# Split products from the tenth early block on, six more blocks ahead of the gates, and the last two Gelus left in PSUM

## The chip, the core and the metric

The kernel runs on one core of a Trainium2 chip. The metric is the device time of one execution in microseconds (us); of three executions of the kernel before, the median is 944.98 us. TensorE is called PE here, VectorE DVE, ScalarE ACT, GpSimd POOL and the queue that issues the DMAs SP, as in the profile.

## What is computed

One transformer layer on 256 tokens: attention and a pooling mixer, a projection, and then a feed-forward part with 16,384 experts, which takes most of the time. The reference of that part, cut:

```python
s1 = einsum('bthd,nd->bthn', q1, sub_keys1); s2 = einsum('bthd,nd->bthn', q2, sub_keys2)
v1, i1 = top_k(s1, 16); v2, i2 = top_k(s2, 16)           # per head, 8 heads, 128 keys each
cand_s = v1[..., :, None] + v2[..., None, :]             # 256 candidates
cand_i = i1[..., :, None] * 128 + i2[..., None, :]
top_s, pos = top_k(cand_s, 16); eid = take_along_axis(cand_i, pos)
gate = softmax(top_s)
a = gelu(einsum('td,tkd->tk', h, peer_u[eid]))
out = einsum('tk,tkd->td', gate * a, peer_v[eid])
```

The kernel gathers nothing: it computes `gelu(h @ peer_u.T)` for all experts, multiplies it with a matrix of gates that is zero where an expert was not picked, and multiplies by all of `peer_v`.

## The kernel before, in words

The experts are cut into 128 blocks of 128. A block has an *up* half (its 128 x 1024 part of `peer_u` times the normed tokens, then Gelu) and a *down* half (the gated result times its part of `peer_v`, 12 matmuls of 512 columns, `down`). The first 108 blocks (`EARLY`) have their up half done early, before the gates exist, and their Gelus are kept in DRAM (`up_dram`) until the down stage reads them back. The other 20 have it done in the late loop, between the down halves (`up`).

An up half comes in two forms. In *full precision* (`early_part`, line 1975) the matmul is fp32. As a *split product* the weights and the tokens are each a high part (a rounded copy) plus a low part (the rest), and three products of them are summed: high by high, high by low, low by high. A narrow split block is 24 matmuls of 256 columns (`split_part`, line 2045), a wide one 8 of 512 and 8 of 256 columns. The high part of a block's weights is a copy by ACT (`early_high`, line 759), the low part a subtraction by DVE or POOL (`early_low`, lines 1325 and 1642). The tokens' own low parts (`low_part` in POOL, line 1558, four pieces, semaphore `p_hlo`) are needed too.

Between 140 and 235 us the *picks* are made, head by head, for 8 heads. PE makes the scores. DVE finds the best keys (`best_keys`, line 1216 and on) and the best pairs (`best_pairs`), compares positions (line 1247), and sums up the expert numbers (`look_up`, line 1255). POOL adds up candidates (`candidates`, `staircase`, line 1563) and multiplies matches by numbers (`matches`, line 1593). `last_matches` (line 1266) is DVE's share of the eighth head's matches; it waits for `p_cide`, which POOL sets after its last staircase. Seven small steps follow in DVE, and then PE transposes the picks (line 2064). PE fills this time with early blocks: 0 to 12 in full precision, 13 and 14 (`SPLIT_E`) as split products.

After that the *gates* are built by one-hot products (`gate_half`, line 2077), with the split blocks 14 to 107 woven in by a fixed count of matmuls (`fill`). Then comes the down stage: 108 down halves, and the late loop.

All of it is in an order written out by hand: each engine runs its own list, and waits on named counters. `e_up` counts finished up halves, `e_gel` Gelus, `eu_hi` and `eu_lo` high and low parts of weights. SP loads each block's weights into a ring of three (`load_ring`, `ld_t`), stores each Gelu (`store_early`), and itself waits in its list for these counters. A Gelu goes into one of two `gel` buffers, and so waits for the store of two blocks before:

```python
act.wait_ge(e_up, e + 1)
if e >= 2:
    act.wait_ge(st_e[e % 2], 16 * (e // 2))
act.activation(gel[:, e % 2, :], psum[:, early_bank(e), 0:SEQ], ACT.Gelu).then_inc(e_gel, 1)
```

## Time and profile before

| | us |
|---|---|
| median of 3 executions | 944.98 (943.74 to 945.27) |
| the profiled execution | 942.8 |
| its span | 941.0 |
| PE busy | 932.4 |
| DVE busy | 770.6 |
| ACT busy | 500.3 |
| POOL busy | 321.2 |

The span runs from the first to the last instruction of the execution; the time of the execution is 1.8 us longer. The granted clock of PE is 1.00 over the whole trace behind its first microseconds. Matmuls are pipelined, so what a block costs is read from the start of one group of matmuls to the start of the next, not from durations.

### The profile page before, as it was taken

The numbers are of one execution on the slowest core, as the hardware profiler recorded it, in microseconds if no ns is written. First come the engines' busy times: TensorE is split into PE (matmuls) and PEld (weight loads), VectorE is DVE, ScalarE is ACT, GpSimd is POOL, SyncE is SP. The second block draws the span as 40 slices with busy tenths as digits, with TensorE's granted clock in tenths as the row PEclk, the third lists the DMA queues.
The fourth block names the chain that finished last, engine by engine and source line by source line (L and its number), as shares of the span: only waits on it lengthen the run. The fifth ranks groups of instructions, "written<-read, shape, count | busy, mean of one in ns | idle before, by whom it ended". The sixth has DMA issues, their size and how long they took to land.

```text
span 941.0 us, 15375 instructions
## 1 busy us (share of the span) xinstructions
PE 932.4 (99%) x5396; PEld 816.7 (87%) x5396; DVE 770.6 (82%) x1450; ACT 500.3 (53%) x872; POOL 321.2 (34%) x292
## 2 busy tenths in 40 slices
PE   9999999999999999999999999999999999999998
PEld 8998899998988888888888888888888888888887
DVE  5899758999886888788778898888888888777776
ACT  6576544433767777777777544334343343343342
POOL 3084228888476766767667000000000000000000
PEclk9999999999999999999999999999999999999999
DMA  9543138826776676667667777787777777766664
GB/s 293 160 135 123 48 99 300 211 78 179 216 245 198 206 218 195 226 195 236 203 200 224 250 246 232 245 242 236 245 236 243 239 237 245 206 219 186 195 193 140
DMA packets 93783, 193.46 MB, mean 206 GB/s; under 512 B 8449, under 2 KB 59265, under 8 KB 93457
## 3 DMA queue, kind: packets, MB, share of 16 engines
q1 hardware_dynamic: 93280, 190.38, 64.8%
q0 software_dynamic: 288, 2.10, 1.2%
q8 instruction: 40, 0.66, 0.3%
q14 instruction: 31, 0.25, 0.1%
q10 hardware_dynamic: 144, 0.08, 0.0%
HBM read 174.43 MB, written 15.99 MB: 202 GB/s over the span
## 4 chain that ended last, share of the span: by engine, by line
PE 95%; ACT 2%; DVE 2%; DMA 1%; issue 0%; DVEq 0%; ACTq 0%
PE psum L2131 37%; PE psum L2051 16%; PE psum L2048 8%; PE psum L1675 5%; PE psum L1975 5%; PE psum L1944 4%; PE psum L2111 4%; PE psum L2077 3%; PE psum L2045 2%; PE psum L1691 2%; PE psum L2114 2%; PE psum L1732 1%; PE psum L1853 1%; PE psum L1969 1%; PE psum L1936 1%; DMA up_kept<-gel 1%
## 5 line engine op out<-in xcount | busy, mean ns | idle before, releaser
L2131 PE MATMUL psum<-rr 128*128 128x512 f32 x1536 | 354.0, 390 | 1.0 <-DVE rr L1399 1.0
L2131 PEld LDWEIGHTS psum<-rr 128*128 128x128 f32 x1536 | 286.0, 188 | 64.6 <-issue 1.1
L851 ACT ACTIVATE rr<-raw 128x1024 fp32r<-128x1024 f32 x105 | 111.7, 1064 | 176.4 <-PE psum L2131 176.2
L1332 DVE TENSOR_TENSOR rr<-raw,rr 128x1024 fp32r<-128x1024 f32 x106 | 129.9, 1225 | 25.9 <-ACT rr L851 25.5
L2051 PE MATMUL psum<-h_all,rr 128*128 128x512 f32 x456 | 123.4, 395 | 0.0
L2051 PEld LDWEIGHTS psum<-h_all,rr 128*128 128x128 f32 x456 | 82.5, 188 | 13.5
L1352 DVE TENSOR_REDUCE gel<-psum 128x256 f32<-128x512 f32 x86 | 58.6, 681 | 14.3 <-DMA up_kept<-gel 12.7
L759 ACT ACTIVATE rr<-raw 128x1024 fp32r<-128x1024 f32 x64 | 67.2, 1050 | 4.7 <-DMA raw<-in_peer_u_dram 4.6
L2051 PE MATMUL psum<-h_all,late_b 128*128 128x512 f32 x232 | 64.8, 394 | 0.0
L1635 POOL TENSOR_TENSOR rr<-raw,h_all 128x640 fp32r<-128x640 bf16 x32 | 40.3, 1259 | 59.0 <-DVE raw L1309 58.7
L1399 DVE TENSOR_TENSOR rr<-big,rr 128x256 fp32r<-128x256 f32 x128 | 54.4, 425 | 4.4
L889 ACT ACTIVATE rr<-raw 128x1024 fp32r<-128x1024 f32 x22 | 23.4, 1062 | 62.0 <-PE psum L2131 61.1
L1393 DVE TENSOR_TENSOR big<-big,gel 128x256 f32<-128x256 f32 (+1 forms) x128 | 53.6, 419 | 2.8 <-ACT gel L750 2.0
L2111 PE MATMUL psum<-h_all,rr 128*128 128x512 f32 x152 | 54.4, 392 | 0.0
L1397 DVE TENSOR_SCALAR rr<-big 128x256 fp32r<-128x256 f32 (+1 forms) x128 | 37.7, 294 | 20.2 <-PE psum L2131 9.7
L845 ACT ACTIVATE big<-psum 128x512 f32<-128x512 f32 x64 | 37.8, 591 | 29.5 <-PE psum L2077 29.3
L745 ACT ACTIVATE gel<-gel 128x256 f32<-128x256 f32 x86 | 35.3, 411 | 31.5 <-DVE gel L1352 30.5
L1635 POOL TENSOR_TENSOR rr<-raw,picks 128x640 fp32r<-128x640 bf16 x32 | 49.1, 1536 | 0.0
L2051 PEld LDWEIGHTS psum<-h_all,late_b 128*128 128x128 f32 x232 | 42.9, 188 | 6.7
L1385 DVE TENSOR_TENSOR rr<-raw,rr 128x1024 fp32r<-128x1024 f32 x22 | 26.9, 1225 | 25.9 <-ACT rr L889 25.9
L1675 PE MATMUL psum<-rr,h_all 128*128 128x256 f32 (+1 forms) x384 | 46.5, 281 | 0.6 <-ACT raw L612 0.6
L1975 PE MATMUL psum<-t32s,raw 128*128 128x256 f32 x208 | 46.7, 379 | 0.0
(240 smaller groups left out, 1766.5 us busy)
## 6 DMA issues: line engine op xcount, KB each, us to landing
raw<-in_peer_v_dram SPq DMA_DIRECT2D x128, 512.0 KB, 3.9
raw<-in_peer_u_dram SPq DMA_DIRECT2D x127, 512.0 KB, 4.2
up_kept<-gel SPq DMA_DIRECT2D x106, 128.0 KB, 3.6
gel<-up_kept SPq DMA_DIRECT2D x106, 128.0 KB, 3.9
big<-in_w_in_dram SPq DMA_DIRECT2D x10, 1024.0 KB, 5.7
big<-in_peer_wq_dram SPq DMA_DIRECT2D x8, 1024.0 KB, 5.5
big<-in_w_out_dram SPq DMA_DIRECT2D x4, 1024.0 KB, 5.3
rr<-big POOLq DMA_DIRECT2D x2, 1024.0 KB, 8.9
```

The lines of the kernel that those rows point to most:

```text
L759: act.activation(early_split(e, 0), u_ring[e % 3].rearrange("p (k n) -> p k n", k=DK), ACT.Copy).then_inc(eu_hi, 1)
L851: act.activation(v_sp[b % 2][:, 0, :], early_v(b), ACT.Copy).then_inc(v_hi, 1)
L1332: dve.tensor_tensor(v_sp[b % 2][:, 1, :], early_v(b), f(v_sp[b % 2][:, 0, :]), ALU.subtract).then_inc(v_lo, 1)
L1352: dve.tensor_reduce(gel[:, e % 2, :], psum[:, early_bank(e), :].rearrange("p (a t) -> p t a", a=2), AX.X, ALU.add).then_inc(e_sum, 1)
L1399: dve.tensor_tensor(g_sp[:, s, 1, :], gates_at(b), f(g_sp[:, s, 0, :]), ALU.subtract).then_inc(g_lo, 1)
L1635: i = pool.tensor_tensor(pairs_at[q % 2][:, 0:n, part, :], cols[q % 2][:, :, :, 0], p.unsqueeze(2).to_broadcast([P, n, NK]), ALU.mult)
L1675: i = pe.matmul(dst, lhs(a, k), rhs(b, k), start=(n == 0), stop=(n == 3 * DK - 1))
L1975: i = pe.matmul(psum[:, early_bank(e), 0:SEQ], u_ring[e % 3][:, k * P:(k + 1) * P], t32s[:, k, :], start=(k == 0), stop=(k == DK - 1))
L2048: i = pe.matmul(bank[:, 0:SEQ], early_split(e, 1)[:, k, :], ht[:, 0, k, :], start=False, stop=False)
L2051: i = pe.matmul(bank.rearrange("p (a t) -> p a t", a=2), early_split(e, 0)[:, k, :], ht[:, :, k, :], start=(k == 0), stop=(k == DK - 1))
L2111: return pe.matmul(both, ut[s][:, 0, k, :], ht[:, :, k, :], start=(k == 0), stop=(k == DK - 1))
L2131: i = pe.matmul(psum[:, 4 + 2 * t + n, :], g_sp[:, s, x, t * P:(t + 1) * P], v_sp[s][:, y, n * 512:(n + 1) * 512], start=(first and m == 0 ...
```

## The change

`EARLY` goes from 108 to 114 and `EARLY_TOP` from 15 to 21: six blocks leave the late loop, and 21 blocks stand ahead of the gates. From block 9 on (`SPLIT0`) all early blocks are split products, so that 9 to 12 change their form and 13 to 18 are new there. The blocks woven between the gates are 94 before and after. What goes with it:

- PE computes blocks 0 to 8 in full precision, 9 to 18 with `split_part`, then as before one block around the transposes. Each of them waits for the Gelu of the block two before (`e_gel`). In block 9 the order of products is changed, so that the token's low parts are needed last.
- ACT copies the tokens' high part one step earlier (in the last head's turn, ahead of `keep_s`), and makes the high parts of blocks 9 to 20 between its Gelus.
- DVE makes the low parts of blocks 9 to 20, between the steps of the picks' last two heads.
- POOL makes the tokens' four low parts ahead of the matches of the sixth head; before, one came after those matches and three after the last.
- SP loads blocks 9 to 11 into space left by the projections' weights (`raw_more`), ahead of time, and 12 on into the ring; from block 12 on a load waits for a low part.
- The last two Gelus (blocks 112 and 113) are written in place in PSUM, and DVE multiplies from there; so they wait for no store, and SP can reload the first two stored Gelus into `gel` as soon as the stores are done.

The core of the diff:

```diff
-EARLY, EARLY_TOP = 108, 15
+EARLY, EARLY_TOP = 114, 21
+SPLIT0 = PH + 1
-EXP_AT = EARLY_TOP - 5
+EXP_AT = SPLIT0 + 4
...
+        raw_more = [wraw.rearrange("p s k n -> p (s k n)")[:, n * D:(n + 1) * D] for n in range(3)]
-        early_sp = [rr[:, n:n + 2 * D].rearrange("p (a k n) -> p a k n", a=2, k=DK) for n in (2 * D, 4 * D)]
+        early_sp = [rr[:, n:n + 2 * D].rearrange("p (a k n) -> p a k n", a=2, k=DK) for n in (2 * D, 4 * D, 6 * D, 0)]
...
             def keep_early(e):
                 sp.wait_ge(e_up, e + 1)
-                load_ring(e + 3)
+                if e < SPLIT0 - 3:
+                    load_ring(e + 3)
+                else:
+                    sp.wait_ge(ld_t[e % 3], 16 * (e // 3 + 2))
+                    load_ring(e + 6)
                 if e:
                     store_early(e - 1)
+                if e == SPLIT0 - 4:
+                    sp.wait_ge(z_done, z_after(N_CHUNK - 1))
+                    for k in range(3):
+                        sp.wait_ge(ld_t[k], 16 * ((SPLIT0 - 3) // 3 + 1))
+                        load_ring(SPLIT0 + k)
...
                 act.wait_ge(e_up, e + 1)
+                if e >= EARLY - 2:
+                    mine = psum[:, early_bank(e), 0:SEQ]
+                    act.activation(mine, mine, ACT.Gelu).then_inc(e_gel, 1)
+                    return
...
+                if h == PH - 1:
+                    act.wait_ge(p_t32, 1)
+                    act.activation(ht[:, 0], t32s, ACT.Copy).then_inc(a_hi, 1)
                 keep_s(h)
...
+            early_high(SPLIT0)
+            early_high(SPLIT0 + 1)
             numbers(PH - 1)
             for e in range(PH - 1, EXP_AT):
                 early_gelu(e)
+                if e < SPLIT0:
+                    early_high(e + 4)
+                elif e > SPLIT0:
+                    early_high(e + 3)
...
                 if h < PH:
                     best_keys(h)
+                if h == PH - 1:
+                    early_low(SPLIT0)
...
                 if h >= 2:
                     best_pairs(h - 1)
+                if h == PH - 1:
+                    early_low(SPLIT0 + 1)
                 if h == PH:
...
                     last_matches()
+                    early_low(SPLIT0 + 4)
                 if h >= 2:
                     look_up(h - 2)
+                if h == PH - 1:
+                    early_low(SPLIT0 + 2)
+                    early_low(SPLIT0 + 3)
+            for e in range(SPLIT0 + 5, SPLIT0 + 8):
+                early_low(e)
             dve.wait_ge(d_seq, seq.n)
             look_up(PH - 1)
+            early_low(SPLIT0 + 8)
...
-            for e in SPLIT_E:
+            for e in range(SPLIT0 + 9, FILL0 + 1):
                 early_low(e)
...
+                if h == PH - 2:
+                    for n in range(N_OUT):
+                        low_part(n)
                 matches(h - 1)
-                if h == PH - 2:
-                    low_part(0)
-            for n in range(1, N_OUT):
-                low_part(n)
...
-            for e in range(PH - 2, EARLY_TOP - 2):
+            for e in range(PH - 2, SPLIT0):
                 early_up(e)
...
                     if n == 0:
                         pe.wait_ge(eu_hi, split_number(e))
+                        if e < FILL0:
+                            pe.wait_ge(e_gel, e - 1)
...
-            pe.wait_ge(e_gel, EARLY_TOP - 3)
             pe.wait_ge(a_hi, 4)
-            pe.wait_ge(p_hlo, N_OUT)
+            for e in range(SPLIT0, SPLIT_E[0]):
+                split_part(e, 0, UNITS)
             split_part(SPLIT_E[0], 0, 2 * DK)
```

In the lists below a row is one instruction with its line, the tile it writes, what it reads, and the counters it waits for. DVE at the end of the picks, before: `L1282` is the step ahead of `last_matches` (`L1266`), `L1255` is `look_up`, `L1290` the first of the small steps, `L1325` a low part of a block's weights.

```order
L1282 TENSOR_TENSOR big<-big 128x256
L1266 TENSOR_TENSOR big<-big 128x800 [waits p_cide,d_match]
L1255 TENSOR_REDUCE big<-big 128x2x16 [waits p_eq]
L1255 TENSOR_REDUCE big<-big 128x2x16 [waits p_eq,d_seq]
L1290 CAST big<-big 128x256 [waits d_pick]
```

The same place after the change, where `L1327`, `L1307`, `L1290` and `L1342` are these steps and `L1300` is a low part:

```order
L1327 TENSOR_TENSOR big<-big 128x256
L1307 TENSOR_TENSOR big<-big 128x800 [waits p_cide,d_match]
L1300 TENSOR_TENSOR rr<-raw,rr 128x1024 [waits eu_hi]
L1290 TENSOR_REDUCE big<-big 128x2x16 [waits p_eq]
L1300 TENSOR_TENSOR rr<-raw,rr 128x1024 [waits eu_hi] x3
L1290 TENSOR_REDUCE big<-big 128x2x16 [waits p_eq,d_seq]
L1300 TENSOR_TENSOR rr<-raw,rr 128x1024 [waits eu_hi]
L1342 CAST big<-big 128x256 [waits d_pick]
```

The low part of block 13 now stands right behind `last_matches`, those of 14 to 16 behind the first `look_up`, that of 17 behind the second. Four more (9 to 12) stand earlier in the same list.

POOL around the matches of the sixth head, before: `L1563` is the end of a staircase, `L1593` and `L1605` the matches, `L1558` a low part of the tokens.

```order
L1593 TENSOR_TENSOR big<-big 128x800 [waits d_match,p_cide,p_seq]
L1593 TENSOR_TENSOR big<-big 128x800
L1605 TENSOR_TENSOR big<-big 128x2x400 [waits p_seq]
L1558 TENSOR_TENSOR h_all<-t32s,h_all 128x2x256 [waits a_hi]
L1563 TENSOR_TENSOR big<-big 128x2x16 [waits d_top]
```

After the change, with `L1607` as the low parts and `L1612`, `L1642`, `L1654` as staircase and matches:

```order
L1607 TENSOR_TENSOR h_all<-t32s,h_all 128x2x256 [waits a_hi] x4
L1612 TENSOR_TENSOR big<-big 128x2x16 [waits n_ev]
...
L1642 TENSOR_TENSOR big<-big 128x800 [waits d_match,p_cide,p_seq]
L1642 TENSOR_TENSOR big<-big 128x800
L1654 TENSOR_TENSOR big<-big 128x2x400 [waits p_seq]
L1612 TENSOR_TENSOR big<-big 128x2x16 [waits d_top]
```

All four low parts of the tokens now stand ahead of the sixth head's staircase and matches.

## Rows read from the trace of the kernel before

**Rows 1.** The page: busy us (share of span) x instructions of each engine.

```profile
PE 932.4 (99%) x5396; PEld 816.7 (87%) x5396; DVE 770.6 (82%) x1450; ACT 500.3 (53%) x872; POOL 321.2 (34%) x292
```

**Rows 2.** PE's waits, longest first: who waited, for whom: us, times, longest.

```profile
PE psum L1719 <- POOL big L1467: 1.0, 1, 1.0
PE psum L2131 <- DVE rr L1399: 1.0, 1, 1.0
```

**Rows 3.** Timeline of PE ahead of the gates: start, us, instruction, [idle before <-releaser].

```profile
208.66 24.34 PE L1975 MATMUL psum<-t32s,raw 128*128 128x256 f32 x112
232.65 2.24 PE L2045 MATMUL psum<-h_all,rr 128*128 128x256 f32 x16
...
245.99 3.01 PE L2045 MATMUL psum<-h_all,late_b 128*128 128x256 f32 x24
248.83 1.10 PE L2045 MATMUL psum<-h_all,rr 128*128 128x256 f32 x8
```

**Rows 4.** Timeline of PE in the late loop.

```profile
829.99 2.91 PE L2131 MATMUL psum<-rr 128*128 128x512 f32 x12
832.73 0.40 PE L2111 MATMUL psum<-h_all,rr 128*128 128x512 f32 x1
...
835.51 2.91 PE L2131 MATMUL psum<-rr 128*128 128x512 f32 x12
```

**Rows 5.** Timelines of PE, ACT and DVE at the start of the down stage.

```profile
527.53 2.97 PE L2045 MATMUL psum<-h_all,late_b 128*128 128x256 f32 x24
531.47 38.76 PE L2131 MATMUL psum<-rr 128*128 128x512 f32 x169 [0.96 <-DVE rr L1399]
...
529.62 0.39 ACT L750 ACTIVATE gel<-psum 128x256 f32<-128x256 f32 x1 [0.96 <-DMA up_kept<-gel]
...
530.11 0.43 DVE L1393 TENSOR_TENSOR big<-big,gel 128x256 f32<-128x256 f32 x1 [1.97 <-ACT gel L750]
```

**Rows 6.** Timeline of POOL in the last three heads of the picks.

```profile
215.44 1.28 POOL L1558 TENSOR_TENSOR h_all<-t32s,h_all 128x512 fp32r<-128x512 f32 x1
...
222.97 2.10 POOL L1563 TENSOR_TENSOR big<-big 128x32 f32<-128x32 f32 x7
225.20 2.37 POOL L1593 TENSOR_TENSOR big<-big 128x800 f32<-128x800 bf16 x1
227.53 3.75 POOL L1558 TENSOR_TENSOR h_all<-t32s,h_all 128x512 fp32r<-128x512 f32 x3
```

**Rows 7.** Timeline of DVE at the end of the picks.

```profile
225.17 0.99 DVE L1266 TENSOR_TENSOR big<-big 128x800 f32<-128x800 bf16 x1 [0.66 <-POOL big L1563]
226.08 5.72 DVE L1255 TENSOR_REDUCE big<-big 128x32 f32<-128x1600 f32 x2
231.83 0.30 DVE L1290 CAST big<-big 128x256 int32<-128x256 f32 x1
...
234.24 2.35 DVE L1325 TENSOR_TENSOR rr<-raw,rr 128x1024 fp32r<-128x1024 f32 x2
```

**Rows 8.** Timelines of DVE and POOL where they work on SBUF at once.

```profile
190.36 2.82 DVE L936 TENSOR_TENSOR rr<-big,rr 128x2048 fp32r<-128x2048 f32 x1 [1.48 <-ACT rr L552]
238.71 2.31 DVE L1325 TENSOR_TENSOR late_c<-raw,rr 128x1024 fp32r<-128x1024 f32 x1
...
189.49 5.11 POOL L1593 TENSOR_TENSOR big<-big 128x800 f32<-128x800 bf16 x2
...
201.27 3.06 POOL L1593 TENSOR_TENSOR big<-big 128x800 f32<-128x800 bf16 x2
...
238.68 1.26 POOL L1635 TENSOR_TENSOR rr<-raw,picks 128x640 fp32r<-128x640 bf16 x1
```

**Rows 9.** Timelines of SP (issue of a weight load) and ACT in the picks.

```profile
226.13 0.33 SPq L436 DMA_DIRECT2D raw<-in_peer_u_dram  x1
...
224.10 1.28 ACT L811 ACT_TABLE_LOAD   x1
229.75 1.06 ACT L759 ACTIVATE rr<-raw 128x1024 fp32r<-128x1024 f32 x1 [0.64 <-DMA raw<-in_peer_u_dram]
```

**Rows 10.** Timeline of PE in the first microseconds.

```profile
1.00 3.44 PE L1719 MATMUL psum<-big 128*128 128x128 f32 x16 [1.00 <-POOL big L1467]
...
6.04 0.83 PE L1719 MATMUL psum<-big 128*128 128x128 f32 x6
```

More of the change, by code:

```diff
@@ L372, in early_split, with early_raw @@
         def early_split(e, part):
-            return early_sp[e - SPLIT_E[0]][:, part] if e in SPLIT_E else split_ring[e % 3][part]
+            return early_sp[(e - SPLIT_E[0]) % 4][:, part] if e <= FILL0 else split_ring[e % 3][part]
+        def early_raw(e):
+            return raw_more[e - SPLIT0] if SPLIT0 <= e < SPLIT0 + 3 else u_ring[e % 3]
         def split_number(e):
-            return e - SPLIT_E[0] + 1
+            return e - SPLIT0 + 1
         def split_low_ready(eng, e):
-            mine = [k for k in range(SPLIT_E[0], e + 1) if pool_low(k) == pool_low(e)]
+            mine = [k for k in range(SPLIT0, e + 1) if pool_low(k) == pool_low(e)]
             eng.wait_ge(ep_lo if pool_low(e) else eu_lo, len(mine))
@@ L469, in _ @@
             load_w(WQ0 + 6)
-            for e in range(SPLIT_E[0]):
+            for e in range(SPLIT0):
                 keep_early(e)
@@ L476, in _ @@
                     load_w(WQ0 + 7)
-            for e in range(SPLIT_E[0], EARLY):
+            for e in range(SPLIT0, EARLY):
                 keep_split(e)
@@ L481, in _ @@
             sp.dma_start(u_first.rearrange("p k n -> p (k n)"), pu[EARLY]).then_inc(ld_uf, 16)
+            for b in range(2):
+                sp.wait_ge(st_e[b], 8 * (EARLY - 2))
+                load_e(b + 2)
             for b in range(EARLY):
-                sp.wait_ge(d_g32, b + 1)
-                if b < 2:
-                    sp.wait_ge(st_e[b], 8 * (EARLY - 2))
-                if b < EARLY - 2:
+                if 2 <= b < EARLY - 2:
+                    sp.wait_ge(d_g32, b + 1)
                     load_e(b + 2)
@@ L758, in early_high @@
                     act.wait_ge(e_up, e - 2)
-                act.activation(early_split(e, 0), u_ring[e % 3].rearrange("p (k n) -> p k n", k=DK), ACT.Copy).then_inc(eu_hi, 1)
+                elif e >= SPLIT0 + 4:
+                    act.wait_ge(e_up, e - 3)
+                act.activation(early_split(e, 0), early_raw(e).rearrange("p (k n) -> p k n", k=DK), ACT.Copy).then_inc(eu_hi, 1)
             def numbers(h):
@@ L801, in _ @@
                     early_gelu(h - 2)
-            act.wait_ge(p_t32, 1)
-            act.activation(ht[:, 0], t32s, ACT.Copy).then_inc(a_hi, 1)
             early_gelu(PH - 2)
@@ L877, in _ @@
                         early_next(e)
+                if c == HALVES - 1:
+                    ring_v(1)
                 if q < NQ:
@@ L1260, in block_u, with early_low @@
                 dve.tensor_tensor(ut[s][:, 1], u_raw[:, s], f(ut[s][:, 0]), ALU.subtract).then_inc(ut_lo, 1)
+            def early_low(e):
+                dve.wait_ge(eu_hi, split_number(e))
+                dve.tensor_tensor(early_split(e, 1), early_raw(e).rearrange("p (k n) -> p k n", k=DK), f(early_split(e, 0)), ALU.subtract)\
+                   .then_inc(eu_lo, 1)
             def last_matches():
@@ L1344, in next_rows @@
             def next_rows(q):
+                if q == 0:
+                    dve.wait_ge(e_up, FILL0 - 2)
                 if q >= RS:
@@ L1392, in block_g @@
                     dve.wait_ge(a_gel, b + 1 - EARLY)
-                dve.tensor_tensor(gates_at(b), gates_at(b), gel[:, s, :], ALU.mult).then_inc(d_g32, 1)
+                up_gelu = psum[:, early_bank(EARLY - 2 + b), 0:SEQ] if early and b < 2 else gel[:, s, :]
+                dve.tensor_tensor(gates_at(b), gates_at(b), up_gelu, ALU.mult).then_inc(d_g32, 1)
                 dve.wait_ge(d_g32, b + 1)
@@ L2040, in split_part @@
                             pe.wait_ge(e_gel, e - 2)
-                    if n == (2 * DK - 2 if wide(e) else 2 * DK):
+                    if e == SPLIT0 and n == 2 * DK:
+                        pe.wait_ge(p_hlo, N_OUT)
+                    if n == (DK if e == SPLIT0 else 2 * DK - 2 if wide(e) else 2 * DK):
                         split_low_ready(pe, e)
```

25 lines of the change are left out of this document (14 added, 11 removed).

## The prediction

> **What bounds the kernel now.** I read the page's busy line first: TensorE (PE) is busy 932.4 of 941.0 us [rows 1]. Then PE's waits: none is longer than 1.0 us, and after the start the longest is that before the first block of the down stage [rows 2]. So PE has work behind work from end to end; an edit gains only by giving PE less of it or by taking out that 1.0 us, and it loses by whatever makes PE wait anew. After that I read the timelines of PE, VectorE (DVE), GpSimd (POOL) and ScalarE (ACT) between 205 and 245 us, where the picks are made, since all of the moved work lands there. The reader should see two things in them: VectorE and GpSimd are both without a gap there, and they hand results to and fro.
>
> **PE's own work.** A block in full precision is 16 matmul records. Seven of them run from 208.66 to 232.65 [rows 3], so one costs 23.99/7 = 3.43 us. A narrow split block is 24 matmuls of 256 columns: 245.99 to 248.83, 2.84 us [rows 3]. An up block in the late loop takes 832.73 to 835.51 = 2.78 us, the down half 829.99 to 832.73 = 2.74 us [rows 4]. By the diff four blocks (9 to 12) go from full precision to split, and six blocks leave the late loop and are computed ahead of the gates as narrow blocks. The 86 wide blocks stay 86, and the blocks woven between the gates stay 94. So PE loses 4 x 3.43 + 6 x 2.78 = 30.4 us and gets 10 x 2.84 = 28.4 us: -2.0 us. All of it lies on PE, which sets the end, so all of it counts. The moved blocks' down halves do not change; their extra store and reload of 128 KB run on queues in which PE does not wait today.
>
> **The start of the down stage.** PE ends its fill at about 530.5 (527.53 plus 24 matmuls) and starts at 531.47 [rows 5]. What came last is ScalarE's Gelu of block 106, which waited 0.96 us for a store to free its `gel` buffer [rows 5]. With the result left in PSUM it waits for no store and can start at about 528.6, behind ScalarE's copy of v; VectorE's three steps behind it (1.2 us, 530.11 to 531.3 today) then end before PE is there. I take the whole 0.96 us: -0.9. If VectorE's reads from PSUM cost more, up to all of it is lost (0).
>
> Together -2.9 us, if nothing new waits. The rest of the working is about that.
>
> **When PE wants the low parts.** Nothing before block 9 moves on PE, so block 9 starts at 208.66 + 3 x 3.43 = 218.95, and block 13 at 218.95 + 4 x 2.84 = 230.3. Its last eight matmuls need its low part, 16 matmuls later: at 232.2.
>
> **When VectorE can have it.** The low part of block 13 stands behind `last_matches`, which waits for GpSimd's last `p_cide`. Today that comes at 222.97 + 2.10 = 225.07 [rows 6], and VectorE had waited 0.66 us for it [rows 7]. GpSimd's work up to there is one unbroken line, and the change puts things into it:
> - Three of its four low parts of the tokens move from behind the matches to ahead of them: 3.75 us [rows 6]. That makes 228.8. (The fourth lay in the line before, at 215.44 [rows 6].)
> - VectorE's four new low parts (blocks 9 to 12). Rows 8 show what a subtraction of two SBUF tiles on VectorE does beside a GpSimd instruction: one waits for the other to end. A subtraction that came at 190.36 in the middle of GpSimd's pair of 800-element products made the pair last 5.11 us where another pair lasts 3.06; a low part at 238.71 lasted 2.31 us, waiting for the GpSimd product that had begun at 238.68, where two low parts in a row last 2.35 us together with nobody beside them [rows 7, 8]. So each low part among GpSimd's line holds that line up by its own length, some 1.15 us: 4 x 1.15 = 4.6. That makes 233.4.
>
> From there the order of today's rows goes on: `last_matches` takes 0.9 us; GpSimd's last product, already waiting, goes next and ends 2.5 us after `p_cide` (225.07 to 225.20 + 2.37 [rows 6]), and the low part, 1.2 us, comes behind it: 233.4 + 2.5 + 1.2 = 237.1. PE wanted it at 232.2, so PE waits about 5.0 us. This takes in the smaller waits of blocks 9 and 10 for their low parts, which push block 13 back but not the chain.
>
> The low part of block 14 stands behind `look_up` of the seventh head, half of 5.72 us [rows 7]: it comes 2.86 + 1.15 = 4.0 us after that of block 13, and PE asks 2.84 us after: +1.2. Blocks 15 to 17 follow 1.15 us apart or have time. The end of the chain (`look_up`, the low part of 17, the seven small steps) comes 2 x 1.15 + 2.86 + 1.15 + 2.4 = 8.7 us after the low part of 14, while PE reaches the transposes 0.95 + 4 x 2.84 + 1.9 = 14.2 us after it; that wait stays hidden.
>
> Bounds of the new waits: none if VectorE and GpSimd held each other up nowhere (below); at the top, 8.7 us, if the moved low parts of GpSimd also hold up the comparisons of VectorE that run at the same time (two, by 1.25 us each: +2.5). I take 6.2, because rows 8 show the hold-up on just these kinds of instruction, and GpSimd's line has no gap to hide it.
>
> The Trainium skill, "SBUF — State Buffer", section "Who interferes with whom", goes further than the rows: it says that any VectorE instruction with two SBUF inputs shuts out a GpSimd instruction that reads SBUF for its whole length, and the other way round. By that VectorE's comparisons of 800 bf16 elements would wait for GpSimd's low parts as well, which no row shows, as they only met the staircase's instructions of 0.3 us (2.10/7 [rows 6]); the sum by it would be up to 2.5 us more.
>
> **Sum.** -2.0 - 0.9 + 5.0 + 1.2 = +3.3 us. The profiled execution took 942.8 us (span 941.0 and 1.8 around it), 2.2 under the median of 944.98; by the profile the new time is 946.1, and against the median 944.98 + 3.3 = 948.3.
>
> **Rivals.**
> - *The chain has room (faster).* If the two engines passed each other freely, GpSimd's line ends at 228.8 and VectorE, today ready for `last_matches` at 225.17 - 0.66 = 224.5, is ready at 224.5 + 4.6 = 229.1: block 13's low part is there at 231.2, a microsecond ahead of PE. What then comes last is ScalarE: the Gelu of block 13 stands behind the load of block 15 (3.6 us from issue to use, 226.13 to 229.75), its copy and two table loads of 1.28 us [rows 9]; the load goes out at about 228.1, so 228.1 + 3.6 + 1.06 + 1.28 + 0.42 + 1.28 + 0.39 = 236.1, and PE asks at 218.95 + 6 x 2.84 = 236.0. That is up to 0.8 us with the stores. -2.9 + 0.8 = -2.1: 942.9. The decision lies at 232.2: the low part of block 13 before or after. Against it: rows 8, and a GpSimd line that has no gap.
> - *Half of it (no change to be seen).* The low parts fall where GpSimd waits for its own results, and take the memory in time that it doesn't use; how many such moments there are, the merged rows do not show. Half of the 4.6 us gone leaves waits of 2 to 4 us: -0.9 to +1.1, about 945.0.
> - *PE's clock falls in the wait.* A wait of 5 us in PE is longer than any in the trace. Its price by rows: at the start, before the clock was granted, 16 matmuls took 3.44 us, and six of the same kind later 0.83 [rows 10]; 3.44 - 16 x 0.83/6 = 1.2 us once, 949.5. The records of this run show no level below full speed after the start, so whether 5 us is enough is open. The Trainium skill, "TensorE: Matmul & The Clock Gate", Part 1, says that an idle PE is gated to half rate again; no row here shows it.
>
> **How the numbers follow.** A measurement of this kernel can tell about 0.2%, 1.9 us, from no change. The hold-up in the chain, with or without the clock: 0.62, slower, 947 to 952. Half of it: 0.20, within 0.2%. Room in the chain: 0.18, faster, 942.9. The forecast is that of the first, 948.3. The range goes from 943.0, which leaves out about half of the last case, to 952.0: -2.9 + 8.7 + 1.2 = +7.0 at the top end.
>
> **What would show it.** In the profile after: PE's waits list a single wait of 4 to 6 us on VectorE's low part of block 13, and one of about 1 us on that of block 14; GpSimd's last `p_cide` ends near 233 and not 225; its pairs of 800-element products last 4 to 5 us where a low part falls between them; the first gate starts 20.9 us later than now (10 x 2.84 - 4 x 3.43 = 14.7 of it work, 6.2 waits). In the down stage the wait of 1.0 us is gone and the late loop is 6 x 2.78 = 16.7 us shorter. The forecast is wrong if low part 13 ends ahead of 232.2, if VectorE's low parts do not lengthen GpSimd's line, or if narrow blocks in this stretch take other than 2.84 us.

## The result and the profile after

The changed kernel takes 947.95 us (median of 8 executions, 946.33 to 949.45), the kernel before 944.62 beside it: a ratio of 1.0035 (95% interval 1.0026 to 1.0045), 3.3 us slower. In a second series the same two kernels gave 946.3 and 943.3, ratio 1.0030 (1.0019 to 1.0041). The profiled execution of after took 948.26 us, 0.3 over its median, while the profiled one of before lies 1.8 under its own; so two profiles laid side by side show more than 3.3.

| start of | before | after | after, second series |
|---|---|---|---|
| first fp32 matmul of the early blocks | 154.22 | 155.02 | 154.35 |
| first gate | 240.79 | 263.19 | 261.56 |
| last gate | 526.47 | 549.59 | 548.23 |
| down stage | 531.47 | 553.46 | 552.10 |
| its last matmul | 937.33 | 942.80 | 941.57 |

All differences below are taken from one start to the next, so what an execution had lost ahead of the early blocks drops out. From the first early block to the first gate the changed kernel takes 21.6 us more (20.6 in the second series); the prediction said 20.9. The gates take 0.7 and 1.0 more, the start of the down stage 1.1 less, the down stage with the late loop 16.5 and 16.4 less: in sum +4.7 and +4.1 against a profile of before that was a short one.

PE's waits in the profile of after (who waited, for whom: us, times, longest), to be laid beside [rows 2], and its timeline (start, us, instruction, [idle before <- releaser]) beside [rows 3]:

```profile
PE psum L2098 <- DVE rr L1300: 3.6, 2, 3.1
...
PE psum L2098 <- ACT gel L776: 0.9, 1, 0.9
```

```profile
209.46 10.53 PE L2022 MATMUL psum<-t32s,raw 128*128 128x256 f32 x48
220.94 1.17 PE L2098 MATMUL psum<-h_all,rr 128*128 128x256 f32 x8 [0.95 <-ACT gel L776]
222.65 12.88 PE L2098 MATMUL psum<-h_all,rr 128*128 128x256 f32 x104 [0.54 <-DVE rr L1300]
238.59 18.91 PE L2098 MATMUL psum<-h_all,rr 128*128 128x256 f32 x144 [3.06 <-DVE rr L1300]
257.34 0.82 PE L2117 MATMUL psum<-cst,big 128*128 128x128 f32 x6
```

Block 9 waits for a Gelu, then for its low part, and at 235.5 block 13 waits 3.06 us for its low part. The last group but one holds a further loss that no list of waits shows: 144 matmuls take 18.75 us to the next group's start, where six times 2.84 us for 24 [rows 3] is 17.0. The granted clock says why (stretch, length, PE busy, PEclk, DMA share, GB/s; after):

```profile
236.00:238.00 2.00, 0.00 (x0) 1.00 0.01 4
238.00:240.00 2.00, 1.41 (x9) 0.81 0.25 41
240.00:242.00 2.00, 2.00 (x11) 0.50 0.76 283
242.00:244.00 2.00, 2.00 (x17) 0.84 0.25 51
244.00:246.00 2.00, 2.00 (x20) 1.00 0.75 278
```

It is 1.00 through the wait, falls to 0.50 (1.2 of 2.4 GHz) shortly after PE has started again, and is back at 1.00 by 244. The three stretches below 1.00 lose 2 x (0.19 + 0.50 + 0.16) = 1.7 us.

VectorE and GpSimd in the picks of after (timelines), to be laid beside [rows 6 to 8]:

```profile
209.55 1.28 DVE L1279 CAST big<-big 128x32 bf16<-128x32 uint32 x1
210.86 3.15 DVE L1282 TENSOR_TENSOR big<-big 128x800 bf16<-128x800 bf16 x2
...
220.06 2.53 DVE L1300 TENSOR_TENSOR rr<-big,rr 128x1024 fp32r<-128x1024 f32 x1
...
229.28 2.58 DVE L1300 TENSOR_TENSOR rr<-raw,rr 128x1024 fp32r<-128x1024 f32 x1
233.53 0.18 DVE L1279 CAST big<-big 128x32 bf16<-128x32 uint32 x1
233.75 1.06 DVE L1282 TENSOR_TENSOR big<-big 128x800 bf16<-128x800 bf16 x2
...
235.06 2.34 DVE L1307 TENSOR_TENSOR big<-big 128x800 f32<-128x800 bf16 x1
237.32 1.21 DVE L1300 TENSOR_TENSOR rr<-raw,rr 128x1024 fp32r<-128x1024 f32 x1
```

```profile
209.53 5.63 POOL L1607 TENSOR_TENSOR h_all<-t32s,h_all 128x512 fp32r<-128x512 f32 x4 [0.32 <-ACT h_all L820]
...
216.48 3.06 POOL L1642 TENSOR_TENSOR big<-big 128x800 f32<-128x800 bf16 x2
...
221.47 4.20 POOL L1612 TENSOR_TENSOR big<-big 128x32 f32<-128x32 f32 x14
225.80 4.97 POOL L1642 TENSOR_TENSOR big<-big 128x800 f32<-128x800 bf16 x2
230.74 2.22 POOL L1612 TENSOR_TENSOR big<-big 128x32 f32<-128x32 f32 x7
234.98 1.57 POOL L1642 TENSOR_TENSOR big<-big 128x800 f32<-128x800 bf16 x1 [2.03 <-DVE big L1282]
```

Read them in pairs, the lines of VectorE with those of GpSimd that run at the same time. Beside GpSimd's four token low parts (209.53 on) VectorE's copy of 32 elements takes 1.28 us, undisturbed 0.18, and its two comparisons 3.15, undisturbed 1.06. Two of the new low parts take 2.5 us, undisturbed 1.2. The other way round GpSimd's pair of products takes 4.97 us beside low parts, undisturbed 3.06, and its last seven staircase steps 2.22, where they take 1.24 in the run with one source, below. The kernel before had a sign of it that is in none of the rows ahead of the prediction: beside GpSimd's products the last head's copy took 0.68 us, in the two heads ahead of it 0.23 and 0.25 (timeline of DVE, before):

```profile
222.37 0.68 DVE L1244 CAST big<-big 128x32 bf16<-128x32 uint32 x1
```

The last `p_cide` comes at 232.96, or at 232.2 with the 0.8 us taken off by which this execution runs behind (predicted 233.4). In this execution VectorE is later still: GpSimd then waits 2.03 us for VectorE's comparisons. In the second series the end is as predicted, although there the low parts hold up the staircase (14 steps in 6.22 us) and not the pair of products (3.07 us): the last `p_cide` comes at 233.19, `last_matches` waits 0.83 us for it, GpSimd's product goes next, and low part 13 is there at 236.8 (predicted 237.1; GpSimd, then VectorE, second series):

```profile
221.73 6.22 POOL L1612 TENSOR_TENSOR big<-big 128x32 f32<-128x32 f32 x14
...
231.11 2.08 POOL L1612 TENSOR_TENSOR big<-big 128x32 f32<-128x32 f32 x7
233.32 2.37 POOL L1642 TENSOR_TENSOR big<-big 128x800 f32<-128x800 bf16 x1
...
233.29 0.99 DVE L1307 TENSOR_TENSOR big<-big 128x800 f32<-128x800 bf16 x1 [0.83 <-POOL big L1612]
234.20 2.57 DVE L1300 TENSOR_TENSOR rr<-raw,rr 128x1024 fp32r<-128x1024 f32 x1
```

At the down stage (timelines of ACT and PE, to lay beside [rows 5]) the Gelu waits for no store, and PE starts without a wait:

```profile
551.35 0.38 ACT L772 ACTIVATE psum<-psum 128x256 f32<-128x256 f32 x1
...
553.46 2.91 PE L2184 MATMUL psum<-rr 128*128 128x512 f32 x12
```

### The profile page after: what moved, and what is told of

The parts are those of the page before. It is cut to its first block, busy times and chain, and to the rows that moved or that the text cites. A ratio compares the mean times of both kernels' runs of the same rounds, so it can differ in the third digit from the quotient of the medians.

```text
span 946.5 us, 15438 instructions
## 1 busy us (share of the span) xinstructions
PE 934.5 (99%) x5476; PEld 821.2 (87%) x5476; DVE 772.8 (82%) x1448; ACT 505.4 (53%) x876; POOL 328.2 (35%) x292
## 4 chain that ended last, share of the span: by engine, by line
PE 68%; DVE 3%; DMA 2%; issue 1%; ACT 1%; POOL 1%; SPq 0%; DVEq 0%; ACTq 0%
PE psum L2184 37%; PE psum L2104 15%; PE psum L2101 8%; PE psum L2130 3%; PE psum L2164 3%; DMA up_kept<-gel 2%; PE psum L2167 1%; PE psum L2098 1%; DVE late_c L1300 1%; DVE rr L1300 0%; ACT rr L787 0%; DVE big L1290 0%; PE psum L1722 0%; DVE big L1510 0%; POOL rr L1682 0%
## 5 line engine op out<-in xcount | busy, mean ns | idle before, releaser
L886 ACT ACTIVATE rr<-raw 128x1024 fp32r<-128x1024 f32 x111 | 118.0, 1063 | 186.0 <-PE psum L2184 186.0
L1378 DVE TENSOR_TENSOR rr<-raw,rr 128x1024 fp32r<-128x1024 f32 x112 | 137.2, 1225 | 27.3 <-ACT rr L886 26.7
L2104 PE MATMUL psum<-h_all,rr 128*128 128x512 f32 x456 | 123.4, 395 | 0.0
L2104 PEld LDWEIGHTS psum<-h_all,rr 128*128 128x128 f32 x456 | 82.5, 188 | 13.5
L787 ACT ACTIVATE rr<-raw 128x1024 fp32r<-128x1024 f32 x71 | 74.6, 1051 | 2.0 <-DMA raw<-in_peer_u_dram 1.9
L2098 PE MATMUL psum<-h_all,rr 128*128 128x256 f32 x392 | 50.6, 287 | 4.7 <-DVE rr L1300 3.6
L1300 DVE TENSOR_TENSOR rr<-raw,rr 128x1024 fp32r<-128x1024 f32 x26 | 38.3, 1480 | 20.1 <-ACT rr L787 20.1
L1446 DVE TENSOR_SCALAR rr<-big 128x256 fp32r<-128x256 f32 (+1 forms) x128 | 37.7, 294 | 20.6 <-PE psum L2184 13.4
L2098 PEld LDWEIGHTS psum<-h_all,rr 128*128 128x128 f32 x392 | 48.8, 194 | 5.8 <-DVE rr L1300 4.3
L1682 POOL TENSOR_TENSOR rr<-raw,picks 128x640 fp32r<-128x640 bf16 x32 | 52.1, 1628 | 0.0
L1722 PEld LDWEIGHTS psum<-rr,h_all 128*128 128x128 f32 (+1 forms) x384 | 44.5, 176 | 2.0 <-issue 1.0
L1372 DVE TENSOR_TENSOR big<-psum,big 128x512 f32<-128x512 f32 x64 | 43.5, 680 | 2.3 <-ACT big L880 2.2
```

What stands on the lines that cost most here:

```text
L787: act.activation(early_split(e, 0), early_raw(e).rearrange("p (k n) -> p k n", k=DK), ACT.Copy).then_inc(eu_hi, 1)
L886: act.activation(v_sp[b % 2][:, 0, :], early_v(b), ACT.Copy).then_inc(v_hi, 1)
L1378: dve.tensor_tensor(v_sp[b % 2][:, 1, :], early_v(b), f(v_sp[b % 2][:, 0, :]), ALU.subtract).then_inc(v_lo, 1)
L1682: i = pool.tensor_tensor(pairs_at[q % 2][:, 0:n, part, :], cols[q % 2][:, :, :, 0], p.unsqueeze(2).to_broadcast([P, n, NK]), ALU.mult)
L1722: i = pe.matmul(dst, lhs(a, k), rhs(b, k), start=(n == 0), stop=(n == 3 * DK - 1))
L2098: i = pe.matmul(bank[:, 0:SEQ], early_split(e, x)[:, k, :], ht[:, y, k, :], start=(n == 0), stop=(n == UNITS - 1))
```

## The experiments

The theory was that of the prediction: VectorE and GpSimd hold each other up on SBUF, and that makes low part 13 late. The main rival was that VectorE's own added time (four low parts of 1.15 us) does it. Ratios are to the kernel before, run on the same chip, with 95% intervals. The waits are those of the profiled execution: "Gelu" is a wait for a Gelu, "low 13" one for the low part of block 13, and "slow clock" says that the granted clock fell to 0.50 behind the wait.

| run | ratio | PE's waits ahead of the gates, us |
|---|---|---|
| changed kernel again (r_after) | 1.0030 (1.0019 to 1.0041) | Gelu 1.1, low 13 3.0, slow clock |
| one-source low parts (e3_onesrc) | 0.9988 (0.9979 to 0.9997) | Gelu 1.3, low 13 1.2, low 14 0.9 |
| token low parts late (e4_tokens) | 0.9999 (0.9990 to 1.0008) | Gelu 1.1, low 13 1.3, low 14 1.0 |
| both (e34_both) | 0.9978 (0.9968 to 0.9987) | Gelu 0.2, low 13 0.2, low 14 1.0 |
| two low parts sooner (e2_order) | 1.0004 (0.9995 to 1.0012) | Gelus 1.3 and 0.9, low parts 0.2, 0.9, 0.4 |
| filled wait (e5_clock) | 1.0034 (1.0022 to 1.0045) | Gelu 1.7, low 14 0.4 |
| Gelus in PSUM alone (e1_gelu) | 0.9997 (0.9989 to 1.0006) | none |
| tokens by DMA (e7_dma) | 1.0069 (1.0055 to 1.0083) | DMA 7.7, slow clock, Gelu 0.5 |
| and reordered (e8_best) | 1.0058 (1.0044 to 1.0072) | DMA 6.8, slow clock |
| block 9 in fp32, DMA sooner (e9_best) | 1.0001 (0.9992 to 1.0010) | Gelu 2.3, slow clock |
| stores sooner (e10_best) | 1.0008 (0.9999 to 1.0018) | Gelus 1.2, 0.5, 2.4, slow clock |
| no DMA (e11_best) | 1.0004 (0.9995 to 1.0013) | low parts 0.7, 2.1 |

**The changed kernel again.** 

> The changed kernel once more, beside the kernel before and the three others of this call. Expected: 3.3 us over the kernel before, ratio 1.0035, with a mean granted clock of 0.996 to 0.998 (one fall or two in the picks).

1.0030, as expected.

**Low parts with one source.**

```diff
+                if e < SPLIT0 + 4:
+                    with nc.allow_low_precision(reason="one element each"):
+                        dve.tensor_reduce(early_split(e, 1), early_raw(e).rearrange("p (k n o) -> p k n o", k=DK, o=1), AX.X, ALU.add).then_inc(eu_lo, 1)
+                    return
```

> The changed kernel in which VectorE makes for blocks 9 to 12, in place of the subtraction of two SBUF tiles, a sum over an axis of length 1: one SBUF source, 1024 elements out as before (the low parts of these four blocks then hold the weights themselves, so values differ). Theory (the two engines hold each other up where VectorE reads two tiles): each of the four takes about 1.1 us and none 2.5; GpSimd's staircase and products beside them keep their lengths; low part 13, at 238.5 now, comes 2 x 1.4 us sooner, at 235.7, PE waits some 0.5 in place of 3.3 and the clock holds: 947.9 - 2.8 - 1.5 - 0.8 (low part 9) = 942.8. GpSimd's token low parts still hold VectorE's copy and comparisons. Rival (only VectorE's own time of 4 x 1.15 us makes it late): no change, 947.9.

The result is the theory's and not the rival's, which had no change. The same number of elements goes through VectorE, and none of these four is held any more (DVE, then POOL):

```profile
219.93 1.19 DVE L1302 TENSOR_REDUCE rr<-big 128x1024 fp32r<-128x1024 f32 x1
...
227.82 1.21 DVE L1302 TENSOR_REDUCE rr<-raw 128x1024 fp32r<-128x1024 f32 x1
...
232.23 2.34 DVE L1311 TENSOR_TENSOR big<-big 128x800 f32<-128x800 bf16 x1
```

```profile
221.31 3.09 POOL L1616 TENSOR_TENSOR big<-big 128x32 f32<-128x32 f32 x14
224.53 3.07 POOL L1646 TENSOR_TENSOR big<-big 128x800 f32<-128x800 bf16 x2
227.56 1.24 POOL L1616 TENSOR_TENSOR big<-big 128x32 f32<-128x32 f32 x7
```

GpSimd's three groups shrink from 4.20, 4.97 and 2.22 us to 3.09, 3.07 and 1.24. Low part 13 ends at 235.7, the clock holds, and the kernel is 4.0 us faster than the changed one. Between the two profiled executions 2.1 us of this lie ahead of the gates, and 1.8 in the gates and the late loop, where nothing was edited; so part of the 4.0 may be scatter. The wait of 13 was 1.2 and not 0.5 because PE asked 0.6 us earlier than expected.

**Token low parts back behind the matches.**

```diff
+                matches(h - 1)
                 if h == PH - 2:
-                    for n in range(N_OUT):
-                        low_part(n)
-                matches(h - 1)
+                    low_part(0)
+
+            for n in range(1, N_OUT):
+                low_part(n)
...
```

> The changed kernel with three of GpSimd's four token low parts back behind the last product, the first behind the matches of the sixth head, as in the kernel before. So that nobody has to wait for them, the second product of blocks 9 to 18 takes the tokens' high part in place of the low part (as many matmuls of the same shape; values differ in these blocks). Theory: GpSimd's line is what low part 13 waits for, so it comes 3 x 1.4 = 4.2 us sooner, and some 2 us more since VectorE's comparisons no longer wait for the token low parts; PE asked 3.3 us before it came: that wait goes, with it the slow clock (1.5), and the wait of 0.8 for low part 9: 947.95 - 5.6 = 942.3. Rival (the four new low parts and the list of VectorE alone make it late): low part 13 comes as late as now, 947.2 to 948.

A gain, but 2.9 us against r_after and not 5.6. The copy and the comparisons are at 0.18 to 0.23 and 1.1 us again. What the expectation overlooked: the token low parts, now behind GpSimd's last product, hold up low part 13 itself (232.29, 2.31 us), and two new low parts are still held (223.08, 2.57 us; and one of 1.67 us):

```profile
223.08 2.57 DVE L1300 TENSOR_TENSOR rr<-big,rr 128x1024 fp32r<-128x1024 f32 x1
...
230.03 2.34 DVE L1307 TENSOR_TENSOR big<-big 128x800 f32<-128x800 bf16 x1
232.29 2.31 DVE L1300 TENSOR_TENSOR rr<-raw,rr 128x1024 fp32r<-128x1024 f32 x1
...
231.48 5.53 POOL L1607 TENSOR_TENSOR h_all<-t32s,h_all 128x512 fp32r<-128x512 f32 x3
```

**Both.** 

> The changed kernel with both at once: the four low parts of blocks 9 to 12 as sums over an axis of length 1 (one SBUF source), and the tokens' low parts back behind the matches, with the second product of blocks 9 to 18 on the tokens' high part (both leave the low parts' share of these blocks out, so values differ). VectorE keeps its own added time of 4 x 1.15 us, and no instruction in the stretch should be held. Each of the two alone left 1.2 to 1.3 us of the 3.0 to 3.3 us at low part 13 and 0.9 to 1.0 at 14. Theory (the hold-ups are the cause, and they add up): the wait at 13 is gone, 14 keeps up to 0.9, the Gelu ahead of block 9 keeps its 1.1: 942.1 - 1.2 = 940.9, ratio 0.9975. Rival (1.2 us come from VectorE's own time): as each alone, 942.1, ratio 0.9988, with the same 1.2 at 13.

0.9978: 2.1 us faster than before and 4.9 faster than the changed kernel (ratio 1.0030 against 0.9978); between the two profiled executions 4.2 us of this lie ahead of the gates. `last_matches` starts here at 228.90, in after at 235.06, and the two runs with one half each lie between, at 232.23 (one source) and 230.03 (token low parts late). With each execution's own start taken off (-0.33 us for the last of these, 0.57, 0.80 and 0.66 for this run, after and the run with one source) that is 228.3, 234.3, 231.6 and 230.4. Taking out one half of the hold-up gives 2.7 us, the other half 3.9, both 5.9: they nearly add up. What is left of VectorE's delay against before (224.5) is 3.8 us. That is about its own added time, four low parts that take 1.13 us each from start to start, less some 0.5 us by which the copy at 222.37 was held in before. So the hold-ups are 5.9 of 9.7 us; measured against r_after, where `last_matches` starts at 233.29 (0.13 off), they are 4.8 of 8.7.

With that gone PE hardly waits for 13 (0.2 us). Against the expectation two instructions are still held, `last_matches` itself beside GpSimd's last product (2.35 us, 0.99 in the second series of after) and low part 13 beside the token low parts (2.32 us; DVE, then POOL):

```profile
228.90 2.35 DVE L1311 TENSOR_TENSOR big<-big 128x800 f32<-128x800 bf16 x1
231.17 2.32 DVE L1304 TENSOR_TENSOR rr<-raw,rr 128x1024 fp32r<-128x1024 f32 x1
...
230.35 5.55 POOL L1611 TENSOR_TENSOR h_all<-t32s,h_all 128x512 fp32r<-128x512 f32 x3
```

And PE waits at the start of the down stage, for the Gelu left in PSUM: ScalarE's copy of v ahead of it had waited 0.79 us for a load.

```profile
PE psum L2190 <- ACT psum L772: 0.5, 1, 0.5
```

**Two low parts sooner.**

```diff
                     last_matches()
-                    early_low(SPLIT0 + 4)
+                    early_low(SPLIT0 + 6)
...
                     early_low(SPLIT0 + 3)
-
-            for e in range(SPLIT0 + 5, SPLIT0 + 8):
+                    early_low(SPLIT0 + 4)
+                    early_low(SPLIT0 + 5)
+
+            for e in range(SPLIT0 + 7, SPLIT0 + 8):
```

> The changed kernel with the low parts of blocks 13 and 14 taken out from behind last_matches and made right behind those of 11 and 12; those of 15 and 16 take their places. Low part 13 ended at 238.5 behind last_matches; now 15 is there, two low parts later. Theory (each low part holds GpSimd's line up by its own length as well): low part 15 ends 2 x 1.15 + 2 x 1.15 = 4.6 us later than 13 did, at 243.2, and PE asks for it at 235.5 + 2 x 2.84 = 241.2, wait 2.0, and 16 comes 1.2 us late behind look_up; without the slow clock: 947.95 - 3.3 - 1.5 + 3.2 = 946.3. Rival (only VectorE's own time counts): 15 ends at 240.9, no wait; 16 is 1.0 late: 947.95 - 3.3 - 1.5 + 1.0 = 944.1.

1.0004, 944.3 us: an order alone takes back 2.5 us of the 3. Low part 15, in the place of 13, ended at 239.9, 3.1 us later than 13 in r_after; that is between the theory's 4.6 and the rival's 2.3, and so is the time, +0.4 us against the kernel before where the theory had +1.7 and the rival -0.5. It does not decide between them, because the new order changed more than the place of two low parts: one of the two low parts took 2.40 us beside a GpSimd product, VectorE had waited 1.61 us for ScalarE's high part ahead of it, and the last head's comparisons, 2.35 us in r_after, took 1.06. No wait was as long as 1.4 us, and the clock stayed at 1.00.

**A filled wait.**

```diff
+                    if e == SPLIT0 + 4 and n == 2 * DK:
+                        pe.wait_ge(s_ev, 2 * PH)
+                        for j in range(24):
+                            pe.matmul(psum[:, 4, 0:SEQ], early_split(e, 0)[:, j % DK, :], ht[:, 0, j % DK, :], start=True, stop=True)
```

> The changed kernel with 24 matmuls more in PE's list, between the first 16 of block 13 and the last 8, into a bank that nobody reads; they take 24 x 0.118 = 2.8 of the 3.1 us in which PE waits for low part 13. Theory: the clock then doesn't fall, and the 16 matmuls behind it that took 0.213 us take 0.118: 947.95 - 1.5 = 946.4, granted clock 1.0 over 239 to 243. Rival: the slow matmuls only filled time in which PE would have waited for low part 14 (it ended at 242.4, PE at full speed asks at 241.4): 947.95 - 0.5 = 947.4. Third: the matmuls are slow for another reason and stay so: 947.9.

The clock holds (PE busy, PEclk, DMA share, GB/s):

```profile
238.00:240.00 2.00, 2.00 (x20) 1.00 0.72 266
240.00:242.00 2.00, 1.56 (x14) 1.00 0.31 72
```

So the fall was caused by the pause. From the start of block 13's last eight matmuls to the transposes PE now takes 17.8 us (237.27 to 255.06), in r_after 18.7 (236.83 to 255.55): 0.9 us less, since a wait of 0.44 us for low part 14 comes out that the slow matmuls had covered. But the filling ran past the arrival of low part 13, at 236.64. Counted from that arrival it is 18.4 us, in r_after 18.8 (from 236.77): 0.4 us, and that is about the rival's price (0.5). In the time itself (946.59, ratio 1.0034 with an interval of 0.23%) a gain of that size can't be seen; that there is one rests on the trace alone.

**The Gelus in PSUM alone**, on the kernel before: the `early_gelu`, `load_e`, `block_g` and `ring_v` lines of the diff. 

> The kernel before with only the last two Gelus in PSUM. By the prediction's term the wait of 0.96 us ahead of the down stage goes and nothing comes in its place: 944.6 - 1.0 = 943.6, a ratio of 0.9990. Rival: the product that VectorE now reads from PSUM, or the loads of the first two stored Gelus, come last there: 944.6, ratio 1.0000, with a wait of the same size on VectorE or on a load.

The wait goes: from the last gate to the down stage 3.87 us, before 4.99. The time, 0.9997, allows anything from -1.0 to +0.6 us. In the profiled execution the gates took 0.9 us more than in that of before, with no edit there. 0.7 to 1.0 us of the kind show in three other profiled executions (after, r_after, e2), 0.3 in e4, and none in eight; where the trace names a releaser, it is a low part made by GpSimd. Which executions have it stays open.

**Looking for a faster version.** First the tokens' low parts without GpSimd's four subtractions:

```diff
-                    for n in range(N_OUT):
-                        low_part(n)
+                    pool.wait_ge(ht_neg, 1)
+                    pool.dma_start(f(ht[:, 1]), t32s, accum_op=ALU.add).then_inc(p_hlo, 16)
...
```

> The changed kernel in which GpSimd doesn't subtract the tokens' low parts: ScalarE writes the negative of the high part (2 us, behind keep_s of the last head) and one DMA, issued by GpSimd ahead of the matches of the sixth head, adds the tokens to it; and SP stores a Gelu ahead of its wait for the loads of blocks 9 and on. Theory: VectorE's copy and comparisons are no longer held (1.05 + 2.1 us) and GpSimd's line is 5.6 - 1.0 us shorter, so low part 13 comes some 3.2 us sooner, and the wait of 1.2 at the start of block 9 goes: 947.9 - 3.2 - 1.5 (clock) - 1.2 = 942.0, with waits of about 1 us each left at 13 and 14, which stand behind VectorE's own four low parts. Rival: the DMA lands too late for block 9 (8.4 us from issue is the median of the same kind of DMA; issued at 210 to 214, wanted at 222): PE waits some us there, 944 to 947; second rival: ScalarE's 2 us delay the picks by as much, and nothing is gained at 13.

> As the kernel with the DMA for the tokens' low parts, and with VectorE's and ScalarE's lists in another order: low part 13 right behind 12; 14 and 15 behind last_matches; 16 and 17 behind look_up of the seventh head; 18 behind the last look_up; ScalarE's Exp with its two table loads after the Gelu of block 13 and not before it, the high part of block 16 behind the Gelu of 14. Theory: every low part then comes before PE asks (13 at about 229 for 233.0, 14 and 15 by 237 for 235.8 and 238.7, 16 by 241 for 241.5, 17 by 242.2 for 244.3, 18 by 246.2 for 247.2), but for about 1 us at 14, and the end of the picks for 250: what stays is the gain of PE's work and the Gelus in PSUM, -2.0 - 1.0 + 1.0 = 2.0 below the kernel before. Rival: the waits go to Gelus and high parts of ScalarE, 1 to 3 us: within 0.2% of the kernel before.

The first rival of e7 came true. The DMA was taken for one like that of the projections, and is not (page of e7, DMA issues: KB, median us from issue to landing):

```profile
rr<-big POOLq DMA_DIRECT2D x2, 1024.0 KB, 9.8
...
h_all<-t32s POOLq DMA_DIRECT2D x1, 1024.0 KB, 17.0
```

```profile
PE psum L2101 <- DMA h_all<-t32s: 7.7, 1, 7.7
```

As many bytes take 17.0 us and not 9.8. The DMA's packets are of 1 KB here and of 8 KB there, and three weight loads run beside it; which of the two counts wasn't tried. Behind that wait, e8's list leaves PE without another up to the gates.

> A version meant to be faster than both: block 9 goes back to full precision (+0.6 us of PE, one low part less in VectorE); the tokens' low parts by the DMA, whose negative part ScalarE now makes straight from the tokens ahead of keep_s, 3 us sooner than in the two kernels with the DMA before; blocks 10 and 11 do their two high products first and the tokens' low part at the end of both, so that it is wanted at 226.1 and not 222; low part 13 stands behind the comparisons, ahead of last_matches, then 14 and 15, look_up, 16 and 17, look_up, 18; Exp after the Gelu of block 13; from block 6 on SP stores a Gelu ahead of its wait for the next block. The DMA took 16.9 us from issue to use; issued at 208.6 it is there at 225.5 to 226. Theory: no wait above 0.5 us; -2.0 + 0.6 - 1.1 = 2.5 below the kernel before, ratio 0.9973. Rival: the DMA shares the queues with three loads of 512 KB and two stores and is there later than 228: waits of 2 us and more, 943 to 945; second rival: ScalarE's 2 us ahead of keep_s delay the keys of the last head, and with it low part 14: 942 to 943.

> As the version before it (block 9 in full precision, the tokens' low parts by the early DMA, the new order in VectorE, ScalarE and SP), and SP now issues the stores of the Gelus 5 and 6 ahead of its load of block 11, where before they stood behind that load and two waits. In the run before PE waited 2.3 us ahead of block 9 for the Gelu of block 7, which waited 3.1 us for the store of 5, and block 9 then took 5.0 in place of 3.4 us, at the lower clock. Theory: both go, 943.8 - 2.3 - 1.6 = 939.9, ratio 0.9960, no wait of PE above 0.5 us between 205 and 260 and the first gate at about 255.8. Rival: the stores share the DMA engines with three loads and the DMA of the tokens and land no sooner, so the wait stays: 943.8, or it moves to block 10 (Gelu of 8) or to the tokens' low parts, which are then wanted at 226: 941 to 943.

In e9 the DMA is in time, but block 9 waits 2.3 us: the Gelu of block 7, which itself waited 3.1 us for a store, ends at 221.25. Then the granted clock falls to 0.50, and the block takes 5.0 us (221.40 to 226.42) and not 3.43. The loads of blocks 9 to 11 beside the DMA took 7.4 us from issue to landing, 5.8 in after, and the stores stand in the same queues. In e10 the stores go out sooner, the loads land later (9.5 us from issue to landing, and ScalarE waits 5.8 us for one), and PE waits for three Gelus: the rival came true.

> A version without a DMA for the tokens' low parts. From the changed kernel: block 9 goes back to full precision (PE +0.6 us, one low part less in VectorE); GpSimd makes the tokens' low parts behind the staircase of the sixth head and not ahead of it, so that VectorE's copy and comparisons of that head are over when they begin; VectorE's list ends with the comparisons, low 13, last_matches, 14, 15, both look_ups, 16, 17, 18; ScalarE's Exp stands behind the Gelu of block 13, and the high part of 16 behind the Gelu of 14; SP stores the Gelus 5 and 6 ahead of its load of block 11. Theory: VectorE loses 2.1 to 3.1 us of hold-up and 2.5 us of low part 9; low part 13 is then there at about 229 to 232 for 232.7, no wait of PE above 0.5 us and no fall of the clock: -2.0 + 0.6 - 1.1 = 2.5 below the kernel before, ratio 0.9973, up to 1 us less gain for small waits. Rival: the four token low parts now hold up something else in VectorE's list or delay the products of the sixth head by 1.2 us more, and 13 is late by 1 to 2 us: 942.5 to 944. Second rival: Gelus that wait for stores ahead of block 9 (up to 1.2 us) stay: 942.2.

The wait for the Gelu ahead of block 9 is gone, with the store of Gelu 5 sooner and VectorE's list less held. But the order has a fault of its own: both `look_up` stand ahead of low part 16, which comes 2.1 us late.

```profile
222.10 13.52 PE L2100 MATMUL psum<-h_all,rr 128*128 128x256 f32 x112
236.27 5.91 PE L2100 MATMUL psum<-h_all,rr 128*128 128x256 f32 x48 [0.66 <-DVE rr L1305]
244.26 1.92 PE L2100 MATMUL psum<-h_all,rr 128*128 128x256 f32 x14 [2.08 <-DVE rr L1305]
```

Its executions fall into two groups: the four with a mean granted clock of 0.999 or 1.000 took 942.2 to 942.6 us, the seven with 0.998 took 943.8 to 945.1. How much of the difference is the clock and how much a longer wait ahead of its fall is not shown, since the one profiled execution is of the first group. No version that computes the whole beats the kernel before; low part 16 ahead of the last `look_up` wasn't tried.

## Why the prediction was right, point by point

- *PE's own work* (-2.0): right. In the run with both halves of the hold-up out the stretch up to the first gate is 16.4 us longer than before. Three waits make 2.1 us of that, read from the start of the last matmul ahead of a wait and so with PE's restart behind it; it leaves 14.3, predicted 14.7, and 0.2 of what is missing lies at the transposes. Down stage and late loop: -16.5, predicted -16.7.
- *The start of the down stage* (-0.9): right in the trace, -1.1, in after and in most of the runs; -0.5 where the load of v came late (e34). In the time it can't be told.
- *Low part 13* (+5.0, with the small waits of 9 and 10): right in cause and nearly in size: 3.2 + 1.4 us in the second series, 3.3 + 2.4 in the first, restarts included. The path was the predicted one in the second series; in the first VectorE's line came last, not GpSimd's. Both lines grow by the hold-up and end within some 2 us of each other, so either can be last; the prediction had put the hold-up on GpSimd's alone.
- *GpSimd's moved token low parts* were thought to delay GpSimd alone, with their hold-up of VectorE's comparisons only in the upper bound. They do hold them up: 1.1 us at the copy and 2.1 at the comparisons. The prediction found no row with a comparison held; the copy of 0.68 us, just ahead of one in the same timeline, was held by GpSimd's products. The Trainium skill, "SBUF — State Buffer", section "Who interferes with whom", said so of two-input instructions: by it the bound was the value to take. The trace agrees (3.15 us against 1.06 for the two comparisons), and it agrees that a reduction is not held (1.2 us in e3). It did not add 2.5 us to the sum: it fell on VectorE's line, and in the second series GpSimd's came last all the same.
- *Low part 14* (+1.2): this step failed in form. It is late in the four runs that keep its place and hold the clock (0.4 to 1.0 us), but in the changed kernel the slow matmuls cover it. In its place stands the slow clock, a rival of its own in the prediction, priced at 1.2 us; the rows show 1.7 gross, and 0.4 to 0.9 net of the wait it covers. So that rival came true together with the forecast, and replaced a term of it. Its price was read from matmuls "before the clock was granted" [rows 10]; but over those microseconds, too, the granted clock of the trace is 1.00, so that the rows show slow matmuls there and not at which clock.
- *"Queues in which PE does not wait"*: wrong. SP's loads of blocks 9 to 11 and its wait for them stand ahead of the store of Gelu 5, and block 9 starts some 1.2 us late: in the second series ScalarE waits 1.25 us for that store; in the first its Gelu stands behind `numbers`, which waits for VectorE's held list. In e11, with the store ahead of the last of these loads and other changes, the wait is gone; in e34, with SP's order unchanged, it is 0.2 us. So what share of it is the order's is not shown.
- *Half of it* and *room in the chain*: both lost. The run with both halves of the hold-up out is the second of these, 0.9978, and it comes out where that rival put it: 2.1 us under the kernel before (predicted 942.9 against 944.98). The size is in part chance, since the waits that are left there (the Gelus ahead of block 9 and the down stage, low part 14) are not those of the rival.

The right total is in part luck: the waits up to the gates came to 6.9 and 5.9 us for 6.2 predicted, but made up of other pieces, and the gates lost up to 1 us that nobody had forecast.

## What to carry to other kernels

In this kernel VectorE and GpSimd had to be costed as one line: a VectorE subtraction or comparison of two SBUF tiles counts in GpSimd's time as well, and GpSimd's work in VectorE's (4.97 us for 3.06, 3.15 for 1.06), while a reduction of as many elements did not (1.2 us each). An order alone was worth 2.5 of the 3 us. And when the prediction speaks of a wait of some microseconds in PE, price the clock with it; but look first which later wait the slow matmuls will cover.

## What was not expected of the hardware

- A copy of 32 elements per partition on VectorE, 0.18 us, took 1.28 us beside GpSimd's subtractions of 1.4 us each: what is held need not be large.
- PE's clock fell to half behind pauses of 2.3 to 7.7 us in every profiled execution that had one (after, r_after, e7 to e10), and in none of those whose longest was 2.1 us or less (e2, e3, e4, e34, e5, e11). Seven other executions of e11 have a mean granted clock of 0.998, so what one profiled execution shows does not hold for all of a kernel.
- A DMA that adds 1 MB into SBUF in packets of 1 KB took 16 to 20 us (e7 to e10), about twice the 8 to 10 us of one in packets of 8 KB, and the weight loads beside it took 5.5 to 9.5 us, without it 5.8 to 6.2. Whether the packets or the traffic beside it make the difference wasn't tried.
